# Block-attention heads scored in pairs: the two row halves of TensorE, two PSUM banks in turn

## The chip, the core and the metric

The program runs on one core of a Trainium2 chip, in one launch. The time is the device time of that core in microseconds (us). The kernel before took 803.91 us, the median of three runs (803.74 to 804.02).

## The reference, cut to what matters

The whole computation is two blocks on 256 tokens of width 1024: a first block with block attention ("moba", 8 heads of 64), retention (4 heads of 128), attention to a memory (4 heads of 128) and a convolutional FFN, and a second block with an mLSTM and a pooling branch and a latent attention. The change touches only the scores of the 8 moba heads. With 256 tokens there is one block, so no past block is ever picked, and what is left is causal attention inside the block with a bias that depends on the distance:

```
s_own = jnp.einsum('bhqd,bhnd->bhqn', q_c, k_own) * dh ** -0.5 + table[:, rel_bucket(d_own)]
s_own = jnp.where(d_own >= 0, s_own, NEG_INF)          # dh = 64, 8 heads, 256 tokens
p = jax.nn.softmax(logits, axis=-1)
y_a = einsum('bhqn,bhne->bhqe', p_own, v_own)          # then y_a @ w_br_attn
```

In the kernel the scores of one head are a lower triangle of blocks: queries 0 to 127 against keys 0 to 127 (128 columns), and queries 128 to 255 against keys 0 to 255 (256 columns), 384 columns in all (`TRI`). Scale, bias and causal mask are one step, since the bias table holds -1e30 above the diagonal.

## The kernel before

All weights come as "pieces" of 128 x 2048 fp32 (1 MB), in the order in which they are multiplied, into a ring of three buffers `raw`. ScalarE (ACT) rounds a piece to `whi` (L1158), VectorE (DVE) takes the rest, `wlo` = `raw` - `whi` (L1661), and TensorE (PE) multiplies each block three times (L488 to L490: high by high, low by high, high by low), so that the sum has nearly fp32 accuracy. Sync (SP) loads the next piece into a buffer once its `wlo` is made (L468). A step p of the program is the work on piece p: 24 matmuls of 128 x 512 on PE for a piece of this stage.

The order is written by hand, engine by engine, as a loop over p. The small work of the attention heads is placed at the start of the steps, as a pipeline over four of them. In step p PE does, in this order: `head_weigh(p)` (head p-3: probabilities times values, into bank `A[3]`), `head_prob_turn(p)` (head p-2: transposes the probabilities, bank `A[2]`), `head_score(p)` (head p-1: the scores, bank `A[1]`) and `head_turn(p)` (the head of step p: transposes queries and keys, bank `A[0]`), and then the matmuls of piece p. The moba heads 0 to 7 have the steps 10 to 17, the retention heads 18 to 21, the memory heads 22 to 25; so moba head h is scored in step 11 + h. Two moba heads of 64 channels lie side by side in 128, so one transpose serves both: `head_turn` is done for the even head only (`TURNED`), and the even head's queries and keys then stand in partitions (rows) 0 to 63 of `qk_t`, the odd head's in 64 to 127.

In step p DVE does, in `head_dve(p)`: head p-3's division by its sum (L1904, L1907); head p-1's scale, bias and mask out of `A[1]` into `prob` (L1924, L1926) and the two row maxima (L1933); the copy of the transposed queries and keys out of `A[0]` into `qk_t` (L1938, even heads only); and behind these the split of piece p+2 (L1661). ACT does the exponentials of head p-1 (L1311) and copies head p-2's transposed probabilities (L1303).

Semaphores that matter: `s_js` counts heads scored (PE to DVE), `s_jse` heads biased (DVE to PE and ACT), `s_jt` and `s_jte` transposes made and copied. An fp32 matmul of this program is carried out as two instruction pairs, so a score matmul is two weight loads (PEld) and two matmuls (PE) in the trace.

Of the kernel before, what the change touches and what calls it, by code (L numbers as in the profile page):

```python
# [11 lines left out]
ALU = mybir.AluOpType  # L12
ACT = mybir.ActivationFunctionType
AX = mybir.AxisListType.X

P = 128
D = 1024
S = 256
# [9 lines left out]
MOBA_H, RET_H, MEM_H, ML_H, MLA_H = 8, 4, 4, 4, 8  # L28
TRI = 384
# [123 lines left out]
def job(kind, h):  # L153
    return JOBS.index((kind, h))


SMAX = [j for j in range(len(JOBS)) if JOBS[j][0] != "ret"]
# [3 lines left out]
def program(nc, ins, out):  # L161
    ctx = ExitStack()
    with ctx:
# [6 lines left out]
        def overlay(size, *groups):  # L170
# [68 lines left out]
        nmax = sb("nmax", [P, 4, T])  # L239
# [24 lines left out]
        A = [ctx.enter_context(nc.psum_tensor(f"head{i}", [P, 512], F32)) for i in range(4)]  # L264
# [16 lines left out]
        s_x, s_par, s_mem, s_c1, s_c2, s_gfin, s_pos, s_rel = (sem(n) for n in (  # L281
            "x_loaded", "params_loaded", "mem_loaded", "consts1_loaded", "consts2_loaded",
            "gfin_loaded", "positions_loaded", "rel_loaded"))
# [9 lines left out]
        s_rb, s_rbs, s_rbd, s_bias = (sem(n) for n in (  # L293
            "rel_rows", "rel_rows_copied", "rel_rows_stored", "bias_loaded"))
        s_jt, s_jte, s_js, s_jse, s_jx, s_jp, s_jpe, s_jo, s_jn = (sem(n) for n in (
            "head_turned", "head_turned_copied", "head_scored", "scores_biased", "probs_ready",
            "probs_turned", "probs_turned_copied", "head_weighed", "head_done"))
# [185 lines left out]
        def _(pe):  # L483
            mm = nc.tensor.matmul
# [166 lines left out]
            def head_turn(p):  # L651

                if head_at(p) is None:
                    return
                kind, h = head_at(p)
                j = job(kind, h)
                if j not in TURNED:
                    return
                n = TURNED.index(j)
                if kind == "moba" and h == 0:  # L660
                    chunk_free(pe, c0("qkv") + 1)
                if kind == "ret" and h == 0:
                    pe.wait_ge(s_rot, 1)
                if kind == "mem" and h == 0:
                    chunk_free(pe, c0("qkv") + 7)
                if n >= 1:
                    pe.wait_ge(s_jte, n)
                else:
                    pe.wait_ge(s_rbs, 1)
                    pe.wait_ge(s_ident, 16)  # L670
                qs, ks = {"moba": (0, 1), "ret": (3, 4), "mem": (7, 8)}[kind]
                c = slice((h // 2 if kind == "moba" else h) * P, (h // 2 if kind == "moba" else h) * P + P)
                for i, s_ in enumerate((qs, ks)):
                    for t in range(T):
                        ins_ = nc.tensor.transpose(A[0][:, i * S + t * P:i * S + t * P + P],  # L675
                                                   tok[:, s_, t, c], ident[:, :])
                ins_.then_inc(s_jt, 1)
# [5 lines left out]
            def head_score(p):  # L683
                if head_at(p - 1) is None:
                    return
                kind, h = head_at(p - 1)
                j = job(kind, h)
                n, qk = turned_buf(j)
                pe.wait_ge(s_jte, n + 1)
                if j >= 1:  # L690
                    pe.wait_ge(s_jse, j)
                if kind == "moba":
                    rows_ = slice((h % 2) * 64, (h % 2) * 64 + 64)
                    mm(A[1][:, 0:P], qk[rows_, 0:P], qk[rows_, S:S + P], start=True, stop=True)
                    i = mm(A[1][:, P:P + S], qk[rows_, P:S], qk[rows_, S:2 * S], start=True, stop=True)
                elif kind == "ret":
                    mm(A[1][:, 0:S], qk[:, S:S + P], qk[:, 0:S], start=True, stop=True)
                    i = mm(A[1][:, S:S + P], qk[:, S + P:2 * S], qk[:, P:S], start=True, stop=True)
                else:
                    for t in range(T):  # L700
                        i = mm(A[1][:, t * S:t * S + S], qk[:, t * P:t * P + P], qk[:, S:2 * S],
                               start=True, stop=True)
                i.then_inc(s_js, 1)
# [942 lines left out]
        def _(dve):  # L1646
            V = nc.vector
            count = [0]

            def order(i):  # L1650

                count[0] += 1
                i.then_inc(s_dve, 1)
                dve.wait_ge(s_dve, count[0])
# [204 lines left out]
            def turn_lo(name, which):  # L1859
                base, _, kbs = fills(name)  # L1860
                hi, lo, d0 = DEST[name]
                for i in which:
# [13 lines left out]
                        last = V.scalar_tensor_tensor(*args, ALU.mult, ALU.subtract)  # L1876
                    last.then_inc(s_tlo, 1)

            def head_dve(p):

                if head_at(p - 3):
                    kind, h = head_at(p - 3)
                    j = job(kind, h)
                    dve.wait_ge(s_jo, j + 1)
                    if kind == "ret":
                        for t in range(T):
                            i = V.bn_stats(bn[:, t, :], A[3][:, t * P:t * P + P])
                        order(i)
                        for t in range(T):
                            i = V.bn_aggr(mv[:, t, :], bn[:, t, :])  # L1890
                        order(i)
                        order(rsqrt(rsum[:, :], mv[:, :, 1], 1.0, T))
                        c = slice(h * P, h * P + P)
                        m = 2 * SUMS.index("mix")
                        order(V.tensor_tensor(rsum[:, :], rsum[:, :], rstd[:, m:m + 2], ALU.mult))
                        for t in range(T):
                            i = V.tensor_scalar(tok[:, 3, t, c], A[3][:, t * P:t * P + P], mv[:, t, 0:1],
                                                rsum[:, t:t + 1], ALU.subtract, ALU.mult)
                        order(i)
                        V.tensor_tensor(tok[:, 3, :, c], tok[:, 3, :, c], tok[:, 6, :, c],  # L1900
                                        ALU.mult).then_inc(s_jn, 1)
                    else:
                        n = SMAX.index(j)
                        order(V.reciprocal(rsum[:, :], psumr[:, n % 4, :]))  # L1904
                        s_, w = (0, 64) if kind == "moba" else (7, P)
                        for t in range(T):
                            i = V.tensor_scalar(tok[:, s_, t, h * w:h * w + w], A[3][:, t * P:t * P + w],  # L1907
                                                rsum[:, t:t + 1], None, ALU.mult)
                        i.then_inc(s_jn, 1)
                if head_at(p - 1):  # L1910
                    kind, h = head_at(p - 1)
                    j = job(kind, h)
                    pr = prob[:, j % 2, :]
                    dve.wait_ge(s_js, j + 1)
                    if kind == "ret":
                        if h == 0:
                            dve.wait_ge(s_c1, 16)
                        V.tensor_tensor(pr[:, 0:TRI], A[1][:, 0:TRI], decay[:, h, :], ALU.mult).then_inc(s_jse, 1)
                    else:
                        n = SMAX.index(j)  # L1920
                        if kind == "moba":
                            if h == 0:
                                dve.wait_ge(s_bias, 16 * MOBA_H)
                            V.scalar_tensor_tensor(pr[:, 0:P], A[1][:, 0:P], 0.125, bias[:, h, P:S],  # L1924
                                                   ALU.mult, ALU.add)
                            order(V.scalar_tensor_tensor(pr[:, P:TRI], A[1][:, P:TRI], 0.125, bias[:, h, :],  # L1926
                                                         ALU.mult, ALU.add))
                            spans = ((0, P), (P, TRI))
                        else:
                            order(V.tensor_scalar(pr, A[1][:, :], P ** -0.5, None, ALU.mult))  # L1930
                            spans = ((0, S), (S, 2 * S))
                        for t, (a, b) in enumerate(spans):
                            i = V.tensor_reduce(nmax[:, n % 4, t:t + 1], pr[:, a:b], AX, ALU.max, negate=True)  # L1933
                        i.then_inc(s_jse, 1)
                if head_at(p) and job(*head_at(p)) in TURNED:
                    n = TURNED.index(job(*head_at(p)))
                    dve.wait_ge(s_jt, n + 1)
                    V.tensor_copy(qk_t[:, n % 2, :], A[0][:, :]).then_inc(s_jte, 1)  # L1938
# [603 lines left out]
```

## Time and profile before

| | |
|---|---|
| median of 3 runs | 803.91 us (803.74 to 804.02) |
| the profiled execution | 803.88 us, of it 802.1 us from the first to the last instruction |
| PE busy | 787.9 us, 98% |
| DVE busy | 562.9 us, 70% |
| ACT busy | 432.6 us, 54% |
| moba heads on PE, steps 10 to 20 | about 64 to 131 us |
| granted TensorE clock | 0.999 of full speed |

The profile is one execution on the chip. PE is the matmul stream of TensorE, PEld its weight loads, which run beside it. Matmuls are pipelined: each row of a timeline gives the start of an instruction and how long it was in flight, so durations of neighbours overlap, and what an instruction costs in a saturated stream is the distance to the next start. The chain of waits gives these costs directly, as it charges each instruction with the time by which it moves the end.

### The profile page before, as it was taken

The numbers are of one execution on the slowest core, as the hardware profiler recorded it, in microseconds if no ns is written. First come the engines' busy times: TensorE is split into PE (matmuls) and PEld (weight loads), VectorE is DVE, ScalarE is ACT, GpSimd is POOL, SyncE is SP. The second block draws the span as 40 slices with busy tenths as digits, with TensorE's granted clock in tenths as the row PEclk, the third lists the DMA queues.
The fourth block names the chain that finished last, engine by engine and source line by source line (L and its number), as shares of the span: only waits on it lengthen the run. The fifth ranks groups of instructions, "written<-read, shape, count | busy, mean of one in ns | idle before, by whom it ended". The sixth has DMA issues, their size and how long they took to land.

```text
span 802.1 us, 11918 instructions
## 1 busy us (share of the span) xinstructions
PE 787.9 (98%) x4616; PEld 689.4 (86%) x4616; DVE 562.9 (70%) x911; ACT 432.6 (54%) x586; POOL 131.2 (16%) x99
## 2 busy tenths in 40 slices
PE   9999999999999999999999999999999999999998
PEld 8787878888888899999988888999799878877776
DVE  5655665895558678787874385689965896887775
ACT  6845454355443566565643364655746345787550
POOL 0002830000000004544441000033005000033000
PEclk9999999999999999999999999999999999999999
DMA  8987344344455465554545535444565324643111
GB/s 336 406 290 262 121 152 158 106 151 165 151 171 202 163 249 209 174 196 168 201 163 204 194 129 203 158 148 162 191 223 181 135 103 159 262 164 138 66 54 53
DMA packets 23364, 142.78 MB, mean 178 GB/s; under 512 B 3564, under 2 KB 4472, under 8 KB 7312
## 3 DMA queue, kind: packets, MB, share of 16 engines
q1 hardware_dynamic: 20160, 134.51, 46.9%
q10 hardware_dynamic: 1776, 4.12, 1.4%
q0 software_dynamic: 1376, 3.43, 1.2%
q8 instruction: 37, 0.61, 0.3%
q14 instruction: 15, 0.12, 0.0%
HBM read 140.97 MB, written 2.64 MB: 179 GB/s over the span
## 4 chain that ended last, share of the span: by engine, by line
PE 84%; DVE 8%; ACT 3%; issue 2%; DMA 2%; SPq 0%; DVEq 0%; ACTq 0%
PE gemm L488 17%; PE gemm L490 16%; PE gemm L489 16%; PE gemm L494 8%; PE gemm L496 8%; PE gemm L495 8%; DVE wlo L1661 2%; DMA raw<-in_weights 2%; ACT whi L1158 2%; DVE xc L2182 1%; PE head L744 1%; PE head L554 1%; PE head L879 1%; PE head L878 1%; PE head L675 1%
## 5 line engine op out<-in xcount | busy, mean ns | idle before, releaser
L1661 DVE TENSOR_TENSOR wlo<-raw,whi 128x2048 fp32r<-128x2048 f32 x121 | 280.8, 2321 | 102.6 <-ACT whi L1158 102.4
L1158 ACT CAST whi<-raw 128x2048 fp32r<-128x2048 f32 x121 | 230.7, 1907 | 195.6 <-PE gemm L490 116.1
L488 PE MATMUL gemm<-whi,x0hi 128*128 128x512 f32 (+2 forms) x400 | 157.2, 393 | 1.4 <-DVE wlo L1661 1.4
L490 PE MATMUL gemm<-whi,x0lo 128*128 128x512 f32 (+2 forms) x400 | 154.0, 385 | 0.0
L489 PE MATMUL gemm<-wlo,x0hi 128*128 128x512 f32 (+2 forms) x400 | 153.7, 384 | 0.0
L494 PE MATMUL gemm<-x1hi,whi 128*128 128x256 f32 x400 | 113.7, 284 | 0.0
L496 PE MATMUL gemm<-x1hi,wlo 128*128 128x256 f32 x400 | 113.3, 283 | 0.0
L495 PE MATMUL gemm<-x1lo,whi 128*128 128x256 f32 x400 | 113.3, 283 | 0.0
L488 PEld LDWEIGHTS gemm<-whi,x0hi 128*128 128x128 f32 x400 | 75.2, 188 | 17.4 <-DVE wlo L1661 2.2
L490 PEld LDWEIGHTS gemm<-whi,x0lo 128*128 128x128 f32 x400 | 75.1, 188 | 14.9
L489 PEld LDWEIGHTS gemm<-wlo,x0hi 128*128 128x128 f32 x400 | 75.3, 188 | 13.4
L495 PEld LDWEIGHTS gemm<-x1lo,whi 128*128 128x128 f32 x400 | 76.8, 192 | 0.0
L494 PEld LDWEIGHTS gemm<-x1hi,whi 128*128 128x128 f32 x400 | 76.8, 192 | 0.0
L496 PEld LDWEIGHTS gemm<-x1hi,wlo 128*128 128x128 f32 x400 | 76.8, 192 | 0.0
L2343 POOL TENSOR_TENSOR ubuf<-gbuf,ubuf 128x512 f32<-128x512 f32 x11 | 33.4, 3035 | 220.1 <-DVE ubuf L2182 220.1
L494 PE MATMUL gemm<-x0hi,whi 128*128 128x256 f32 x192 | 54.7, 285 | 0.5 <-DVE om L2226 0.5
L496 PE MATMUL gemm<-x0hi,wlo 128*128 128x256 f32 x192 | 54.4, 283 | 0.0
L495 PE MATMUL gemm<-x0lo,whi 128*128 128x256 f32 x192 | 54.4, 283 | 0.0
L494 PEld LDWEIGHTS gemm<-x0hi,whi 128*128 128x128 f32 x192 | 36.9, 192 | 0.6 <-issue 0.5
L495 PEld LDWEIGHTS gemm<-x0lo,whi 128*128 128x128 f32 x192 | 36.9, 192 | 0.1
L496 PEld LDWEIGHTS gemm<-x0hi,wlo 128*128 128x128 f32 x192 | 36.9, 192 | 0.0
L488 PE MATMUL gemm<-whi,hthi 128*128 128x512 f32 x88 | 34.4, 391 | 1.0 <-DVE u_up L2220 1.0
(352 smaller groups left out, 1336.5 us busy)
## 6 DMA issues: line engine op xcount, KB each, us to landing
raw<-in_weights SPq DMA_DIRECT2D x122, 1024.0 KB, 4.7
raw<-in_weights SPq DMA_DIRECT2D x4, 512.0 KB, 6.5
bias_rows<-bias_row POOLq DMA_DIRECT2D x1, 1536.0 KB, 19.4
memt<-in_memt SPq DMA_DIRECT2D x4, 256.0 KB, 5.4
tok<-in_mem SPq DMA_DIRECT2D x1, 1024.0 KB, 7.1
xt<-in_xt SPq DMA_DIRECT2D x2, 512.0 KB, 10.9
xres<-in_x ACTq DMA_DIRECT2D x1, 1024.0 KB, 8.6
bias<-bias_rows POOLq DMA_DIRECT2D x8, 128.0 KB, 6.0
```

The lines of the kernel that those rows point to most:

```text
L488: mm(o, xh, wh, start=start, stop=False)
L489: mm(o, xh, wl, start=False, stop=False)
L490: return mm(o, xl, wh, start=False, stop=stop)
L494: mm(o, wh, xh, start=start, stop=False)
L495: mm(o, wh, xl, start=False, stop=False)
L496: return mm(o, wl, xh, start=False, stop=stop)
L554: ins_ = nc.tensor.transpose(b[:, j * S + t * P:j * S + t * P + P], turn_source(name, t, 2 * i + j), ident[:, :])
L675: ins_ = nc.tensor.transpose(A[0][:, i * S + t * P:i * S + t * P + P], tok[:, s_, t, c], ident[:, :])
L744: last = mm(A[3][:, t * P:t * P + w], buf[:, col:col + P], tok[:, vs, k, h * w:h * w + w], start=k == 0, stop=i + 1 == len(src) or src[i + ...
L1158: nc.scalar.copy(whi[:, p % RING, :], raw[:, p % RING, :]).then_inc(s_hi, 1)
L1661: V.tensor_tensor(wlo[:, p % RING, :], raw[:, p % RING, :], whi[:, p % RING, :].bitcast(F32), ALU.subtract).then_inc(s_lo, 1)
L2343: Q.tensor_tensor(u, gbuf[:, i % 2, :, :], u, ALU.mult).then_inc(s_h, 1)
```

## The change

Three edits. On PE, `head_score` does nothing for an odd moba head; for an even one it scores this head and the next, the even head on rows 0 to 63 into `A[1]`, the odd head on rows 64 to 127 into `A[0]`, alternating: the 128-column matmul of each, then the 256-column matmul of each. On DVE the bias step is now a function, `head_bias(kind, h)`; it reads `A[0]` for an odd moba head, and `head_dve` calls it for both heads of the pair in the step of the even one. Since `A[0]` is also the bank of `head_turn`, this one now waits until all heads scored so far are biased (`s_jse`).

```diff
             def head_turn(p):
...
                 if n >= 1:
                     pe.wait_ge(s_jte, n)
+                    if kind == "moba" or kind == "ret" and h == 0:
+                        pe.wait_ge(s_jse, job(kind, h))
...
             def head_score(p):
...
                 if kind == "moba":
-                    rows_ = slice((h % 2) * 64, (h % 2) * 64 + 64)
-                    mm(A[1][:, 0:P], qk[rows_, 0:P], qk[rows_, S:S + P], start=True, stop=True)
-                    i = mm(A[1][:, P:P + S], qk[rows_, P:S], qk[rows_, S:2 * S], start=True, stop=True)
+                    if h % 2:
+                        return
+                    pair = ((A[1], slice(0, 64)), (A[0], slice(64, 128)))
+                    for o, rows_ in pair:
+                        mm(o[:, 0:P], qk[rows_, 0:P], qk[rows_, S:S + P], start=True, stop=True)
+                    for o, rows_ in pair:
+                        i = mm(o[:, P:P + S], qk[rows_, P:S], qk[rows_, S:2 * S], start=True, stop=True)
+                        if o is A[1]:
+                            i.then_inc(s_js, 1)
...
+            def head_bias(kind, h):
+                j = job(kind, h)
+                scores = A[0] if kind == "moba" and h % 2 else A[1]
+                pr = prob[:, j % 2, :]
+                dve.wait_ge(s_js, j + 1)
...
+                        V.scalar_tensor_tensor(pr[:, 0:P], scores[:, 0:P], 0.125, bias[:, h, P:S],
+                                               ALU.mult, ALU.add)
+                        order(V.scalar_tensor_tensor(pr[:, P:TRI], scores[:, P:TRI], 0.125, bias[:, h, :],
+                                                     ALU.mult, ALU.add))
+                        spans = ((0, P), (P, TRI))
...
             def head_dve(p):
...
                 if head_at(p - 1):
                     kind, h = head_at(p - 1)
-                    j = job(kind, h)
-                    pr = prob[:, j % 2, :]
-                    dve.wait_ge(s_js, j + 1)
...
+                    if kind != "moba" or h % 2 == 0:
+                        head_bias(kind, h)
+                    if kind == "moba" and h % 2 == 0:
+                        head_bias(kind, h + 1)
```

The instructions on PE at the start of step 11, before. `head0` to `head3` are the banks `A[0]` to `A[3]`, `gemm0` to `gemm3` those of the pieces; a row here is a matmul of the program (two instruction pairs in the trace, where it is fp32).

```order
L490 MATMUL gemm3<-whi,x0lo 128x512
L694 MATMUL head1<-qk_t 128x128 [waits head_turned_copied]
L695 MATMUL head1<-qk_t 128x256
L488 MATMUL gemm2<-whi,x0hi 128x512 [waits lo_ready]
L489 MATMUL gemm2<-wlo,x0hi 128x512
```

The same place after the change:

```order
L490 MATMUL gemm3<-whi,x0lo 128x512
L699 MATMUL head1<-qk_t 128x128 [waits head_turned_copied]
L699 MATMUL head0<-qk_t 128x128
L701 MATMUL head1<-qk_t 128x256
L701 MATMUL head0<-qk_t 128x256
L488 MATMUL gemm2<-whi,x0hi 128x512 [waits lo_ready]
```

Two matmuls of the odd head have come in, between those of the even head, and the first and last neighbours are the same. The steps 13, 15 and 17 change in the same way.

PE at the start of step 12, before (head 1 is scored, heads 2 and 3 are transposed):

```order
L720 MATMUL head2<-ident,prob 128x128 [waits probs_ready]
L720 MATMUL head2<-ident,prob 128x128 x2
L694 MATMUL head1<-qk_t 128x128 [waits scores_biased,head_turned_copied]
L695 MATMUL head1<-qk_t 128x256
L675 MATMUL head0<-ident,tok 128x128 [waits head_turned_copied]
L675 MATMUL head0<-ident,tok 128x128 x3
L488 MATMUL gemm0<-whi,x0hi 128x512 [waits chunk_emptied_by_act,lo_ready]
```

The same place after the change:

```order
L728 MATMUL head2<-ident,prob 128x128 [waits probs_ready]
L728 MATMUL head2<-ident,prob 128x128 x2
L677 MATMUL head0<-ident,tok 128x128 [waits head_turned_copied,scores_biased]
L677 MATMUL head0<-ident,tok 128x128 x3
L488 MATMUL gemm0<-whi,x0hi 128x512 [waits chunk_emptied_by_act,lo_ready]
```

The scores have left this step (and the steps 14, 16 and 18), so that transposes now stand next to transposes, and the second group has one more wait.

DVE from step 11 on, before (the bias of head 0, a split, the bias of head 1, a copy, a split):

```order
L1924 SCALAR_TENSOR_TENSOR prob<-head1,bias 128x128 [waits bias_loaded,head_scored]
L1926 SCALAR_TENSOR_TENSOR prob<-head1,bias 128x256
L1933 TENSOR_REDUCE nmax<-prob 128x1 [waits dve_own_order]
L1933 TENSOR_REDUCE nmax<-prob 128x1
L1661 TENSOR_TENSOR wlo<-raw,whi 128x2048 [waits hi_ready]
L1924 SCALAR_TENSOR_TENSOR prob<-head1,bias 128x128 [waits head_scored]
L1926 SCALAR_TENSOR_TENSOR prob<-head1,bias 128x256
L1933 TENSOR_REDUCE nmax<-prob 128x1 [waits dve_own_order]
L1933 TENSOR_REDUCE nmax<-prob 128x1
L1938 COPY qk_t<-head0 128x512 [waits head_turned]
L1661 TENSOR_TENSOR wlo<-raw,whi 128x2048 [waits hi_ready]
```

The same place after the change:

```order
L1901 SCALAR_TENSOR_TENSOR prob<-head1,bias 128x128 [waits bias_loaded,head_scored]
L1903 SCALAR_TENSOR_TENSOR prob<-head1,bias 128x256
L1910 TENSOR_REDUCE nmax<-prob 128x1 [waits dve_own_order]
L1910 TENSOR_REDUCE nmax<-prob 128x1
L1901 SCALAR_TENSOR_TENSOR prob<-head0,bias 128x128 [waits head_scored]
L1903 SCALAR_TENSOR_TENSOR prob<-head0,bias 128x256
L1910 TENSOR_REDUCE nmax<-prob 128x1 [waits dve_own_order]
L1910 TENSOR_REDUCE nmax<-prob 128x1
L1669 TENSOR_TENSOR wlo<-raw,whi 128x2048 [waits hi_ready]
L1953 COPY qk_t<-head0 128x512 [waits head_turned]
L1669 TENSOR_TENSOR wlo<-raw,whi 128x2048 [waits hi_ready]
```

The four instructions of head 1 have moved ahead of the split of step 11; DVE still has as many instructions as before. ACT, GpSimd (POOL) and SP keep their order.

## Rows read from the trace of the kernel before

**Rows 1.** Page, busy time by engine: us (share of span) xinstructions
```profile
PE 787.9 (98%) x4616; PEld 689.4 (86%) x4616; DVE 562.9 (70%) x911; ACT 432.6 (54%) x586; POOL 131.2 (16%) x99
```

**Rows 2.** Windows, 60 to 131 us: length, busy by engine, clock, DMA share, GB/s
```profile
60.00:131.00 71.00, 71.00 (x354) 57.28 (x353) 41.75 (x67) 34.90 (x60) 29.54 (x33) 1.00 0.47 166
```

**Rows 3.** Groups by shape, PE, 60 to 131 us: line, op, xcount | busy, mean ns
```profile
L695 PE MATMUL head<-qk_t 64*128 64x256 f32 x16 | 4.8, 377 | 0.0
L694 PE MATMUL head<-qk_t 64*128 64x128 f32 x16 | 3.9, 323 | 0.0
```

**Rows 4.** Chain of waits, step 12: start us, us charged, what
```profile
77.25 0.33 PE head L720 x3
77.58 0.41 PE head L694 x2
78.00 0.43 PE head L695 x2
78.43 0.59 PE head L675 x4
79.02 0.23 PE gemm L488
79.25 0.23 PE gemm L489
```

**Rows 5.** Chain of waits, step 19, a retention head scored on all 128 rows
```profile
131.12 0.33 PE head L720 x3
131.45 0.43 PE head L697 x2
131.88 0.22 PE head L698 x2
132.10 0.44 PE head L675 x4
132.54 0.23 PE gemm L488
```

**Rows 6.** Chain of waits, latent attention, 128-row and 64-row matmuls in turn
```profile
745.09 0.22 PE head L878 x2
745.31 0.41 PE head L879 x2
745.73 0.63 PE head L878 x2
```

**Rows 7.** Timelines, weight loads and matmuls, step 11: start us, us in flight, engine
```profile
70.66 0.18 PEld L694 LDWEIGHTS head<-qk_t 64*128 64x128 f32 x1 [0.35 <-issue]
70.76 0.19 PEld L694 LDWEIGHTS head<-qk_t 64*128 64x128 f32 x1
70.87 0.19 PEld L695 LDWEIGHTS head<-qk_t 64*128 64x128 f32 x1
70.87 0.27 PE L694 MATMUL head<-qk_t 64*128 64x128 f32 x1
70.98 0.19 PEld L695 LDWEIGHTS head<-qk_t 64*128 64x128 f32 x1
71.20 0.38 PE L695 MATMUL head<-qk_t 64*128 64x256 f32 x1
71.51 0.50 PE L488 MATMUL gemm<-whi,x0hi 128*128 128x512 f32 x1
```

**Rows 8.** Timeline, DVE, steps 13 and 14
```profile
86.34 0.29 DVE L1924 SCALAR_TENSOR_TENSOR prob<-head,bias 128x128 f32<-128x128 f32 x1 [0.51 <-PE head L695]
...
87.52 2.60 DVE L1661 TENSOR_TENSOR wlo<-raw,whi 128x2048 fp32r<-128x2048 f32 x1
92.64 0.17 DVE L1904 RECIPROCAL rsum<-psumr 128x2 f32<-128x2 f32 x1 [2.52 <-PE head L744]
```

**Rows 9.** Chain of waits, start of step 14
```profile
93.79 0.59 PE head L675 x4
```

**Rows 10.** Waits of SP, 60 to 131 us: waited for, us, times, longest
```profile
SPq L468 <- DVE wlo L1661: 64.3, 10, 8.9
```

**Rows 11.** Timeline, ACT, step 13
```profile
87.64 0.40 ACT L1311 ACTIVATE prob<-prob,nmax 128x128 f32<-128x128 f32 x1 [0.77 <-DVE nmax L1933]
```

**Rows 12.** Waits of PE, whole span, the longest kind
```profile
PE gemm L488 <- DVE wlo L1661: 3.2, 4, 1.4
```

More of the change, by code:

```diff
@@ L1877, in turn_lo @@
                     last.then_inc(s_tlo, 1)
+            def head_bias(kind, h):
[3 more added lines that the diff above has]
+                dve.wait_ge(s_js, j + 1)
+                if kind == "ret":
+                    if h == 0:
+                        dve.wait_ge(s_c1, 16)
+                    V.tensor_tensor(pr[:, 0:TRI], scores[:, 0:TRI], decay[:, h, :], ALU.mult).then_inc(s_jse, 1)
+                else:
+                    n = SMAX.index(j)
+                    if kind == "moba":
+                        if h == 0:
+                            dve.wait_ge(s_bias, 16 * MOBA_H)
+                        V.scalar_tensor_tensor(pr[:, 0:P], scores[:, 0:P], 0.125, bias[:, h, P:S],
[3 more added lines that the diff above has]
+                        spans = ((0, P), (P, TRI))
+                    else:
+                        order(V.tensor_scalar(pr, scores[:, :], P ** -0.5, None, ALU.mult))
+                        spans = ((0, S), (S, 2 * S))
+                    for t, (a, b) in enumerate(spans):
+                        i = V.tensor_reduce(nmax[:, n % 4, t:t + 1], pr[:, a:b], AX, ALU.max, negate=True)
+                    i.then_inc(s_jse, 1)
             def head_dve(p):
@@ L1911, in head_dve @@
                     kind, h = head_at(p - 1)
-                    j = job(kind, h)
-                    pr = prob[:, j % 2, :]
-                    dve.wait_ge(s_js, j + 1)
[L1915 to L1934, printed above, removed]
+                    if kind != "moba" or h % 2 == 0:
+                        head_bias(kind, h)
+                    if kind == "moba" and h % 2 == 0:
+                        head_bias(kind, h + 1)
                 if head_at(p) and job(*head_at(p)) in TURNED:
```

## The prediction

> **What bounds the kernel now.** I read the busy times first: PE is busy 98% of the span, DVE 70%, ACT 54% [rows 1]. Then the stage: from 60 to 131 us, in which all moba heads lie, PE is busy 71.00 of 71.00 us at the full clock, DVE 41.75, ACT 34.90 [rows 2]. So here every piece of time taken out of PE's own stream is taken out of the end, and work of DVE and ACT costs nothing as long as it is not late. The waits say the same from the other side: SP stands 64.3 us of this stage waiting for `wlo`, with single waits of up to 8.9 us, so loads have room [rows 10], and over the whole span PE's longest kind of wait is 3.2 us in 4 places [rows 12]. Last I read the chain of waits around a score, because it charges each matmul with the time by which it moves what follows: that is the price list of this prediction.
>
> **What the change takes out.** The scores of the heads 1, 3, 5 and 7 leave the steps 12, 14, 16 and 18. In step 12 the chain goes from the transposes L720 at 77.25 to the second gemm matmul at 79.25, 2.00 us [rows 4]. Without scores the same neighbours are 0.33 (L720) + 0.44 (L675 where 128-row work is ahead of it) + 0.23 (L488) = 1.00 us [rows 5]. So a single score costs 1.00 us of PE. What is it made of? The retention head has the same two sizes, a 256-column and a 128-column matmul of two instructions each, on all 128 rows: 0.43 + 0.22 = 0.65 us [rows 5]. The other 0.35 us are paid for going from 128-row to 64-row work and back: L694 takes 0.41 where 0.22 is the stream (0.19), and the transposes behind it 0.59 where 0.44 is the stream (0.15) [rows 4, 5]. The latent attention shows the same surcharge at each such switch: 0.41 for 0.22, and 0.63 for 0.43 [rows 6]. All four odd heads have the same neighbours (L720 ahead, L675 behind; step 14 shows the 0.59 again [rows 9]), so 4 x 1.00 = 4.0 us go. The counts fit: 16 instructions of each kind for 8 heads [rows 3].
>
> **What it adds.** In the steps 11, 13, 15 and 17 the pair has 8 instructions instead of 4, all on 64 rows, so the two switches are shared. If the odd head's streams simply stand behind the even head's, that adds 0.65 us per pair, and no more. If some of them run at the same time on the other row half, it is less. Call the streams in their order a1 a2 (even head, 128 columns), b1 b2 (odd), c1 c2 (even, 256 columns), d1 d2 (odd). Matmuls of one half follow each other; only three neighbours are on different halves: a2 with b1, b2 with c1, c2 with d1. A weight load must come before each. In the rows loads start at 70.66, 70.76, 70.87 and 70.98, one every 0.11 us, though the array has only 64 rows in use [rows 7]. A 128-column stream is 0.11 us too (half of 0.22 [rows 5]). So with one load at a time the small neighbours gain nothing: b1 is ready just when a2 ends. Only c2 with d1 can overlap, streams of 0.21 us (half of 0.43). There are two bounds. In the rows a load begins when the matmul ahead of it starts to stream (the load of L695 at 70.87, the start of the second L694 at 70.87): then d1 starts 0.11 behind c2 and 0.10 is saved. If the load of d1 goes ahead while c1 still streams, since its half of the array is idle, all 0.21 is saved. I take 0.15, the middle, since the trace has no row of two halves side by side: 0.65 - 0.15 = 0.50 us per pair, 4 x 0.50 = 2.0 us added. The ends that I keep for an unknown overlap: below, the case that everything that can neighbour overlaps (0.65 - 0.11 - 0.11 - 0.21 = 0.22 us per pair); above, a surcharge at each change of the half, priced below.
>
> The Trainium skill (TensorE: Matmul & The Clock Gate, "Part 3: Packing small matmuls — row/col tiling") says that matmuls on different row groups run together with a lag of about 4 ns, and that a weight load may go ahead of matmuls in flight where the row group differs. By that rule the whole 0.21 would be saved, and the sum would be 4.0 - 4 x 0.44 = 2.2 us. No row here shows two row halves next to each other.
>
> **Where the rest hides.** DVE gets both biases in the odd steps: one set takes from 86.34 to 87.52, 1.18 us, and the split behind it starts that much later [rows 8]. Nobody waits there: after the split DVE is idle 2.52 us until the weighed head of step 14 [rows 8], so 1.3 us of cover are left. The split itself is for a piece two steps on; behind it stand SP's next load, which has 64.3 us of slack in ten waits, and the multiplication of that piece: two steps last 15.4 us (L675 at 78.43 and 93.79 [rows 4, 9]), so the piece split in step 13 is wanted at about 86.3 + 15.4 = 101.7, and ready at 87.52 + 2.60 + 1.18 = 91.3. In the steps 12, 14, 16 and 18 DVE has 1.18 us less. The new wait in `head_turn`: behind it on PE are the transposes of the next pair and the whole gemm. It needs both biases done: in step 13 about 86.4 + 0.4 + 2 x 1.18, so 89.2, against transposes at 93.8 [rows 9]; 4.6 us of cover. The extra instructions ahead of c2 make the even head's scores 0.2 us late for DVE, and ACT's exponentials (87.64 [rows 11]) as much later; the transposes that need them come in the next step, behind the weighing that releases DVE at 92.64 [rows 8]. The odd head's bias is a step early, which nobody needs. If any of these covers were gone, the price is PE's wait at that place, four times. Behind the stage the work is ordered by semaphores and not by a clock, and PE stays the one that others wait for, so I let the gain through to the end whole.
>
> **The sum.** 4.0 taken out, 2.0 put in: -2.0 us. The profiled execution took 803.88 us (span 802.1), which is the median of the runs but for 0.03, so 801.9 us.
>
> **Rivals.**
> *The halves don't overlap* (the change doesn't do what it says; only switches are saved): -4.0 + 4 x 0.65 = -1.4 us, 802.5. For it: matmuls of fp32 in two instruction pairs each leave only one good neighbour in eight, and no row shows an overlap. Against it: a load does overlap a matmul in flight even on the same rows [rows 7].
> *Loads overlap too*: -4.0 + 4 x 0.22 = -3.1 us, 800.8. For it: 64-row loads use half the array. Against it: the loads in the rows are one every 0.11 us and never two at once [rows 7]. The Trainium skill (TensorEngine Tiling (Array Packing), "Key Properties") says that different tiles can execute weight loads and matmuls in parallel; by that rule this case is the likely one. No row shows it.
> *Each change of the half costs what a switch costs* (the slower side): place, the three changes inside a pair; price 0.19 each, as 128 to 64 rows [rows 4, 6]; the pair then adds 0.65 + 0.57 = 1.22 against 1.00 taken out: +0.22 x 4 = +0.9 us, 804.8. It turns slower from 0.12 us per change on (0.35 / 3). For it: the only changes of the array's use in the trace all cost 0.15 to 0.20. Against it: in all of those the number of rows changes, not their place. The same section of the skill says that a change of the tiling mode drains the array, "not just tile"; by that sentence this case would not happen.
> *DVE becomes late*: the pair of biases would have to take 1.3 us more than priced; I give it nothing but a tail.
>
> **Chances.** Forecast (some overlap, 801.6 to 802.1): 0.44. No overlap, 802.5: 0.26. Loads too, 800.8: 0.14. A cost at each change, 804.8: 0.12. Something else, half of it slower by more: 0.04. A measurement of this kernel can tell about 0.2%, 1.6 us, from no change. Faster by more than that are the forecast and the third case, less a part of the forecast that falls short of 1.6: 0.55. Slower by more needs something beyond the rivals or twice the price of a change: 0.05. The rest, 0.40, is within. The range, 800.6 to 802.9, holds the first three cases, 0.84, with 0.2 to 0.4 us of room on the outside.
>
> **What would show it.** In the changed kernel's trace: 16 instructions of each of the two score lines in four places instead of eight; in step 12 L728 x3, L677 x4 and L488 at 0.33, 0.44 and 0.23 in the chain (the 1.00 is gone); in step 11 the distance from the last gemm matmul of step 10 to the second of step 11 grown by 0.5 us: 0.65 says no overlap, 0.22 says loads too, over 1.0 says that a change of the half costs. The starts of c2 and d1 decide: 0.21 apart, 0.11, or together. The forecast is wrong if the distance grows by more than 0.65, if PE has any wait at L677, or if time comes back later in a wait of PE that the kernel before didn't have.

## The result, and the profile after

The changed kernel takes 799.83 us, the median of six runs (799.63 to 800.27); the kernel before, timed beside it, 803.83 us. The ratio is 0.9948, 95% interval [0.9936, 0.9959]: 4.0 us less, twice the 2.0 us of the forecast, and below the stated range of 800.6 to 802.9. The direction was right and the size was not.

The page's busy times after answer to [rows 1]:

```profile
PE 783.7 (98%) x4616; PEld 686.9 (86%) x4616; DVE 562.9 (71%) x911; ACT 432.6 (54%) x586; POOL 131.3 (16%) x99
```

All instruction counts are as before; DVE, ACT and POOL are as busy as before to 0.1 us; the gain of 4 us is PE's alone (787.9 to 783.7). The groups by shape of the score matmuls between 60 and 131 us answer to [rows 3] (xcount | busy us, mean ns):

```profile
L701 PE MATMUL head<-qk_t 64*128 64x256 f32 x16 | 2.4, 377 | 0.0
L699 PE MATMUL head<-qk_t 64*128 64x128 f32 x16 | 2.0, 322 | 0.0
```

Count (16) and mean duration (377 and 322 ns) are as before, but the time in which such a matmul is in flight has halved, 4.8 to 2.4 and 3.9 to 2.0 us. Each takes as long as it did, and two are in flight at once, all of them.

The chain of waits of step 12, which had 2.00 us from L720 to the second gemm matmul [rows 4]:

```profile
77.19 0.33 PE head L728 x3
77.52 0.43 PE head L677 x4
77.95 0.23 PE gemm L488
78.18 0.23 PE gemm L489
```

That is 0.99 us (78.18 - 77.19); the term "taken out" was right, 1.0 us per pair. The chain of step 11 has the surprise. Before:

```profile
70.50 0.23 PE gemm L490
70.73 0.41 PE head L694 x2
71.14 0.43 PE head L695 x2
71.58 0.43 PE gemm L488
72.00 0.23 PE gemm L489
```

After:

```profile
70.43 0.23 PE gemm L490
70.66 0.42 PE head L699 x4
71.08 0.43 PE head L701 x4
71.51 0.43 PE gemm L488
71.94 0.23 PE gemm L489
```

Four instructions of each size now cost 0.42 and 0.43 us, where two of each cost 0.41 and 0.43. From the last gemm matmul of step 10 to the second of step 11 it is 1.51 us (71.94 - 70.43), and it was 1.50 (72.00 - 70.50): the odd head adds 0.01 us. The gain lies in these steps: in the chain the first score of the retention heads starts at 127.43 us, where it started at 131.45 [rows 5], 4.02 us earlier, and 0.07 of them were there before step 11.

The timeline of the weight loads and the matmuls, in narrow windows (start us, us in flight; x2 are two records in one row), answers to [rows 7]:

```profile
70.58 0.19 PEld L699 LDWEIGHTS head<-qk_t 64*128 64x128 f32 x2 [0.35 <-issue]
70.69 0.19 PEld L699 LDWEIGHTS head<-qk_t 64*128 64x128 f32 x2
70.80 0.20 PEld L701 LDWEIGHTS head<-qk_t 64*128 64x128 f32 x2
70.92 0.19 PEld L701 LDWEIGHTS head<-qk_t 64*128 64x128 f32 x2
```

```profile
70.59 0.38 PE L699 MATMUL head<-qk_t 64*128 64x128 f32 x2
70.80 0.28 PE L699 MATMUL head<-qk_t 64*128 64x128 f32 x2
70.91 0.39 PE L701 MATMUL head<-qk_t 64*128 64x256 f32 x2
71.13 0.38 PE L701 MATMUL head<-qk_t 64*128 64x256 f32 x2
```

The first matmul of the single head, in the kernel before:

```profile
70.66 0.37 PE L694 MATMUL head<-qk_t 64*128 64x128 f32 x1
```

The distances between the starts are those that a single head had: 0.11 us for the loads, 0.21, 0.11 and 0.22 for the matmuls. At each start there are now two loads or two matmuls, at most 0.01 us apart. The row x2 at 70.59 is in flight for 0.38 us together, where the lone one was for 0.37: the second starts with it and doesn't follow it. The last two rows answer the question that the prediction had named as the one that decides: the 256-column streams of the two heads start together.

DVE in the odd steps, which answers to [rows 8] (step 13):

```profile
86.46 0.28 DVE L1901 SCALAR_TENSOR_TENSOR prob<-head,bias 128x128 f32<-128x128 f32 x1
...
87.64 2.45 DVE L1669 TENSOR_TENSOR wlo<-raw,whi 128x2048 fp32r<-128x2048 f32 x1
91.58 0.17 DVE L1938 RECIPROCAL rsum<-psumr 128x2 f32<-128x2 f32 x1 [1.49 <-PE head L752]
```

The second bias takes 1.18 us (86.46 to 87.64), as priced, and 1.49 us of idle time are still left before the next release. PE has no wait at L677. SP still waits 60.2 us for `wlo` in the stage, against 64.3 [rows 10].

### The profile page after: what moved, and what is told of

Read it like the earlier page. It is cut to its first block, busy times and chain, and to the rows that moved or that the text cites. A ratio compares the mean times of both kernels' runs of the same rounds, so it can differ in the third digit from the quotient of the medians.

```text
span 798.2 us, 11921 instructions
## 1 busy us (share of the span) xinstructions
PE 783.7 (98%) x4616; PEld 686.9 (86%) x4616; DVE 562.9 (71%) x911; ACT 432.6 (54%) x586; POOL 131.3 (16%) x99
## 4 chain that ended last, share of the span: by engine, by line
PE 84%; DVE 8%; ACT 3%; issue 2%; DMA 2%; SPq 0%; DVEq 0%; ACTq 0%
PE gemm L488 17%; PE gemm L490 17%; PE gemm L489 16%; PE gemm L494 8%; PE gemm L496 8%; PE gemm L495 8%; DVE wlo L1669 2%; DMA raw<-in_weights 2%; ACT whi L1166 2%; DVE xc L2197 1%; PE head L752 1%; PE head L554 1%; PE head L887 1%; PE head L886 1%; PE head L907 1%
```

## The experiments

Seven kernels ran, each five times or more, beside the kernel before, whose medians were 803.93 us in the first four and 804.17 us in the last three. Expectations and results are told against it unless said otherwise.

**Does the alternation matter?** All of the even head first, then all of the odd head:

```diff
                     for o, rows_ in pair:
                         mm(o[:, 0:P], qk[rows_, 0:P], qk[rows_, S:S + P], start=True, stop=True)
-                    for o, rows_ in pair:
                         i = mm(o[:, P:P + S], qk[rows_, P:S], qk[rows_, S:2 * S], start=True, stop=True)
```

> The changed kernel with the alternation taken out: both matmuls of the even head first (rows 0 to 63, bank A[1]), then both of the odd head (rows 64 to 127, bank A[0]). Theory 1, each row half works through its own matmuls and loads, however far apart the two halves' instructions stand in the program: the odd head still runs beside the even one, the score block of a pair still takes 0.85 us in the chain, and the time is that of the changed kernel, about 4.0 us under the kernel before. Theory 2, matmuls start in program order and only neighbours in the program overlap: of this order only the even head's last 256-column stream and the odd head's first 128-column stream can, 0.11 us per pair, so a pair adds 0.54 us and the kernel is 4 x (1.00 - 0.54) = 1.8 us under the kernel before.

Measured 799.80 us, 4.1 under the kernel before, ratio 0.9947 [0.9934, 0.9961], the same as the changed kernel. The timeline of PE in step 11 (L699 is the 128-column matmul of both heads, L700 the 256-column one). Each row is what is in flight in one narrow window, merged, so the rows overlap: when the first matmul has ended, x4 becomes x3 and the start moves on to that of the next:

```profile
70.56 0.50 PE L699 MATMUL head<-qk_t 64*128 64x128 f32 x4
70.57 0.48 PE L699 MATMUL head<-qk_t 64*128 64x128 f32 x3
70.77 0.28 PE L699 MATMUL head<-qk_t 64*128 64x128 f32 x2
70.88 0.61 PE L700 MATMUL head<-qk_t 64*128 64x256 f32 x4
71.10 0.39 PE L700 MATMUL head<-qk_t 64*128 64x256 f32 x2
```

All four 128-column instructions have started by 70.78, before the first 256-column one at 70.88. But in the program two of them, the odd head's, stand behind the even head's 256-column matmul. So the matmuls of the two halves do not start in program order with respect to each other; it looks as if each half works off its own instructions. Theory 1 holds, theory 2 (program order, 1.8 us) falls, and with it the ground of my sum. The alternation brings nothing that the other order doesn't.

**How much is overlap, and how much shared switches?** The odd head on the same half:

```diff
-                    pair = ((A[1], slice(0, 64)), (A[0], slice(64, 128)))
+                    pair = ((A[1], slice(0, 64)), (A[0], slice(0, 64)))
```

> The changed kernel, but the odd head of each pair is scored on rows 0 to 63 too (from the even head's queries and keys, so heads 1, 3, 5 and 7 come out as other numbers), still into A[0] and in the same places. No two matmuls of a pair are on different halves any more, while the shared switches between 128-row and 64-row work stay. Theory 1 (the gain is overlap of the halves on top of shared switches): a pair adds the plain streams, 0.65 us, and the kernel is 4 x (1.00 - 0.65) = 1.4 us under the kernel before, 2.6 us over the changed kernel. Theory 2 (the gain is in something else, as in fewer waits or in DVE's new order): as fast as the changed kernel, 4.0 us under the kernel before.

Measured 802.37 us, 1.6 under the kernel before, ratio 0.998 [0.9971, 0.9989], and 2.5 over the changed kernel's 799.83. The chain of step 11:

```profile
70.56 0.64 PE head L699 x4
71.19 0.87 PE head L701 x4
```

0.64 + 0.87 = 1.51 us for what costs 0.85 us on two halves: 0.66 us per pair, 2.6 in four, is the overlap, and the rest, 1.6 us measured, comes from sharing the switches. The starts here are one after another (70.49, 70.70, 70.81, 70.92 and so on), as in-order streams should be. Two separate parts, both as large as theory 1 had them.

**Is the surcharge that of 64-row work?** The kernel before, with all 128 rows in each score:

```diff
-                    rows_ = slice((h % 2) * 64, (h % 2) * 64 + 64)
+                    rows_ = slice(0, P)
```

> The kernel before, one head a step, but each moba head is scored on all 128 rows (both heads of the pair summed, so all 8 heads come out as other numbers). This takes away the change between 128-row and 64-row work and nothing else. Theory 1 (each head pays 0.35 us for going to 64 rows and back): 8 x 0.35 = 2.8 us under the kernel before. Theory 2 (the surcharge comes with the score's place, its waits or its bank, and not with the number of rows): no change.

Measured 800.87 us, 3.1 under the kernel before, ratio 0.996 [0.9946, 0.9974]; 0.38 us per head against 0.35. The chain of step 12 has the streams and nothing else:

```profile
77.00 0.22 PE head L694 x2
77.22 0.43 PE head L695 x2
77.66 0.44 PE head L675 x4
78.09 0.23 PE gemm L488
```

0.41 became 0.22 and 0.59 became 0.44, at the same places with the same waits. So what costs is going from 128-row to 64-row work and back: it made a 64-row score 0.35 to 0.38 us dearer than a 128-row one of the same columns.

**Is the DVE part needed?** The odd head's bias back in its own step, PE as changed:

```diff
-                    if kind != "moba" or h % 2 == 0:
-                        head_bias(kind, h)
-                    if kind == "moba" and h % 2 == 0:
-                        head_bias(kind, h + 1)
+                    head_bias(kind, h)
```

> The changed kernel with its DVE part undone: the odd head's scale, bias, mask and maxima stay in the step after the even head's, as in the kernel before, while PE keeps the pairs. Theory 1 (the DVE part is what keeps A[0] free in time): head_turn, which writes A[0] in that same step, waits for them. In step 12 nothing is lost, since DVE has no head to finish there and can bias head 1 early; in the steps 14, 16 and 18 DVE first divides a head (released by the weighing, about 0.85 us) and then biases (1.2 us), so that PE stands about 1.2 us at the transposes: 3 x 1.2 = 3.5 us back, about 0.5 us under the kernel before. Theory 2 (the place of the DVE work does not matter): 4.0 us under the kernel before.

Measured 810.65 us (809.40 to 813.07), 6.7 over the kernel before, ratio 1.0085 [1.007, 1.01]. The mechanism is theory 1's, the loss three times as large as I had it: 10.8 us lost against the changed kernel, not 3.5. The wait of PE over the whole span:

```profile
PE head L677 <- DVE nmax L1910: 7.1, 3, 3.6
```

Three waits, as expected, none in step 12. But they sum to 7.1 us. The chain of the first of them, step 14:

```profile
91.17 0.63 PE head L752 x6
...
93.06 0.62 DVE nmax L1910 x2
...
93.82 0.79 PE head L677 x4
94.60 0.43 PE gemm L488
```

From the end of L752 to the start of L677 it is 2.03 us (93.82 - 91.79). PE spends 0.33 us of them on the transposes L728 and then stands 1.70 us. The longest, 3.6 us in step 18, has more in it: the bias of head 7 also stands behind the emptying of a gate chunk on DVE, which waits for ACT.

```profile
125.83 0.69 ACT tok L1480
...
126.61 1.28 DVE tok L2210 x2
```

And there is a price after the wait: the gemm matmuls that follow cost 0.43 us instead of 0.23. The windows of the steps 14, 16 and 18 (length, PE busy, PEld, DVE, ACT, POOL, clock, DMA share, GB/s) say why:

```profile
93.80:97.60 3.80, 3.78 (x12) 3.12 (x13) 2.92 (x2) 1.71 (x6) 3.72 (x4) 0.55 0.00 0
97.60:103.00 5.40, 5.40 (x34) 4.46 (x33) 0.64 (x3) 1.41 (x1) 5.24 (x8) 1.00 0.56 197
111.00:119.00 8.00, 7.38 (x43) 6.29 (x45) 3.96 (x7) 3.51 (x7) 0.00 (x0) 1.00 0.35 120
128.40:134.80 6.40, 5.00 (x14) 4.16 (x15) 4.11 (x7) 1.26 (x5) 0.00 (x0) 0.50 0.01 3
```

In step 14 the granted clock is 0.55 for 3.8 us, that is 1.2 GHz for nearly all of it, after PE had stood still for 1.70 us among small matmuls, and then full again. In step 16 PE stands just as long, 1.70 us (109.92 to 111.62), and the clock stays at 1.00. In step 18 it is 0.50 for 6.4 us, and the first 1.4 us of them still belong to the wait, which ends at 129.80. So the same wait was followed by a slow stretch once and not the other time, and nothing here says what decides it.

The parts of the loss can be added up in the profiled execution, one of the longer ones: 811.80 us, 11.8 over the 799.99 of the changed kernel's. The waits are 7.1 us. The lower clock takes 1.7 us in step 14 (3.80 x 0.45) and 2.7 us in step 18, counted from the end of the wait (half of the 5.0 us that are left of that window, and 0.2 behind it). That is 11.5, and 0.3 stay open. My 3.5 us had the waits at 1.2 us each, where they were 1.7, 1.7 and 3.6, and no price for the clock.

**The same surcharge elsewhere.** In the latent attention a head's score changes four times between 128 and 64 rows [rows 6]. Both 128-row parts first, then both 64-row parts (the bank's first matmul alone has the start flag, since the parts add up in one bank):

```diff
-                for t, (o, kw) in enumerate((((0), P), ((P), S))):
-                    mm(A[1][:, o:o + kw], qk[:, t * P:t * P + P], qk[:, S:S + kw], start=True, stop=False)
+                blocks = ((0, P), (P, S))
+                for t, (o, kw) in enumerate(blocks):
+                    mm(A[1][:, o:o + kw], qk[:, t * P:t * P + P], qk[:, S:S + kw], start=t == 0, stop=False)
+                for t, (o, kw) in enumerate(blocks):
                     i = mm(A[1][:, o:o + kw], pt[rows_, t * P:t * P + P], pt[rows_, S:S + kw],
-                           start=False, stop=True)
+                           start=False, stop=t == 1)
```

> The changed kernel, with one more edit at another place: in the latent attention a head's score is four matmuls, 128-row and 64-row in turn (two blocks, each a 128-row part and a 64-row part that is added to it). Here both 128-row parts come first, then both 64-row parts: the same instructions, but two changes of the number of rows per head instead of four. Theory 1 (a change of the number of rows costs 0.15 to 0.20 us wherever it stands, and PE bounds this stage too): 8 heads x 0.39 = 3.1 us under the changed kernel, 7.1 us under the kernel before. Theory 2 (the latent attention is bound by its chain through DVE and ACT, so that shorter scores only make PE wait longer for them): less than 1 us under the changed kernel.

> The kernel before with the latent attention's four score matmuls grouped in the same way, and nothing of the change under study. Theory 1 (the two savings are at places that do not touch): 3.1 us under the kernel before, and with the gain of the changed kernel it adds up to the combined one. Theory 2 (the chain through DVE and ACT bounds that stage): less than 1 us.

> The changed kernel as it is, on the same chip as the two grouped ones: 4.0 us under the kernel before.

On one chip: the changed kernel again 799.81 us (0.9947 [0.9934, 0.9961]), the changed kernel with the grouping 797.27 (0.9914 [0.9901, 0.9928]), the kernel before with the grouping 801.28 (0.9966 [0.9952, 0.9979]), the kernel before 804.17. The grouping gives 2.5 us on top of the change and 2.9 without it, where 3.1 was expected. Together 6.9 us against 4.4 + 2.9 = 7.3 apart, so they add up but for 0.4, which is less than the intervals can tell; this is the fastest of all kernels here. The chain of one head, in the changed kernel run again:

```profile
741.11 0.22 PE head L886 x2
741.33 0.41 PE head L887 x2
741.75 0.63 PE head L886 x2
742.38 0.63 PE head L887 x2
743.00 0.59 PE head L860 x4
```

and with the grouping:

```profile
740.41 0.66 PE head L887 x4
741.07 0.85 PE head L889 x4
741.91 0.59 PE head L860 x4
```

2.48 became 2.10 us: 0.38 a head, 3.0 in eight. A new small wait takes part of it back:

```profile
PE head L860 <- DVE olo L2179: 0.5, 3, 0.2
```

3.0 - 0.5 = 2.5. In this stage DVE is close enough behind PE that the last half microsecond shows. The kernel before with the grouping has the same small wait, and by its trace the same gain: from the first transposes of the stage to the end it takes 71.7 us (727.47 to 799.2), where the kernel before takes 74.2 (727.86 to 802.1). The remaining 0.4 of its 2.9 us lie ahead of this stage, where the two kernels are the same, so they are no gain of the grouping.

## Why the prediction was wrong

**What was right.** PE bounds the stage, and what leaves it leaves the end: 4 x 1.00 us taken out of the steps 12, 14, 16 and 18 (0.99 in the chain read above), with all of it there in the time. The parts of this 1.00, stream 0.65 and surcharge 0.35, are shown one by one: sharing the switches gives 1.6 us (1.4 expected), taking them away in eight heads 3.1 (2.8 expected). The covers on DVE held: 1.18 us priced and measured. That the bias must be done early is shown by the kernel in which it isn't.

**What failed.** The term "0.50 us per pair added, 4 x 0.50 = 2.0". It measured 0.01 per pair. Two sentences of the working carried it, and both were wrong. The first: "with one load at a time the small neighbours gain nothing". The rows that I read it from had only one half in use, so they show the pace of loads of one half; with two halves there are two loads at each of the four starts. Even these rows did not say "never two at once": a load starts every 0.11 us and is in flight for 0.18 or 0.19 [rows 7], so that two of one half overlap. The second, which I had not even written down as an assumption: that only "three neighbours are on different halves" could overlap, so that matmuls start in the order of the program. The experiment without the alternation shows the odd head's matmuls running ahead of instructions that stand before them. With the second wrong, even my most favourable rival was too dear: it kept program order, added 0.22 per pair and gave 800.8. If the halves are independent and equally loaded, the pair takes the longer of the two heads, 0 is added, and 803.88 - 4.0 = 799.9, which is the time of the profiled execution, 799.99.

The Trainium skill had the overlap right and the order not. TensorE: Matmul & The Clock Gate, "Part 3: Packing small matmuls — row/col tiling", gives a lag of about 4 ns between matmuls of different row groups; the pairs of starts in the changed kernel are at most 10 ns apart, where loads of one half are 110 ns apart; that agrees, though rows of 10 ns can't tell the 4. It also says that matmuls start and end in program order. The starts in the experiment with head after head are not so, and the measurement decides. TensorEngine Tiling (Array Packing), "Key Properties", says that different tiles carry out loads and matmuls in parallel, which the two loads at each start show; I had let a row of one half weigh more than that, and drew from it a bound for a case that it did not contain.

**The rivals.** "The halves don't overlap" is what the kernel on one half measures, 802.37 against 802.5 forecast, so this case was priced well and didn't happen. A cost at each change of the half is excluded: the pair costs 0.85 us where a single head costs 0.84, and the alternating and the non-alternating order, three changes and one in the program, are equal within 0.03 us. The range missed for one reason: I bounded the added cost by 0.22 from below, where an empty cost, 0, was excluded by nothing in the profile. With 0 as the lower end the range would have reached down to 799.9.

## What to carry to other kernels

Where PE bounds and a contraction is 64 long, put independent work on the two row halves into different banks: the second of the two was free here (0.01 us of 0.65), in both orders that were tried. The two heads had banks of their own in every run; what one shared bank would cost was not run. Keep work of the same number of rows together even where nothing can overlap: going to 64 rows and back costs 0.35 to 0.38 us, and regrouping the four matmuls of each of eight heads was worth 2.5 us without one instruction less. And when a bank gets a second user, do what empties it in the step in which it was filled: left one step later, it cost 10.8 us, waits of PE and a slower clock together.

## What was not expected of the hardware

- Two row halves are served independently, weight loads too: two LDWEIGHTS at 70.58 and two at 70.69, where one half alone gets one every 0.11 us; and a half's first matmul starts at 70.57 although three matmul instructions that start between 70.77 and 71.11 stand before it in the program. The records don't say which half a row belongs to; that the two at one start are one of each half is inferred from the kernel on one half, where no two start together.
- A wait of 1.70 us of PE between transposes was followed by 3.8 us at a granted clock of 0.55, which added 0.20 us to each of seven gemm matmuls. A second wait of 1.70 us at the same place two steps later was followed by none: from 111 to 119 us the clock is 1.00.
